# Applying the RMS factor behind the products at five layer boundaries of a three-model kernel

## The reference

```
def rms_norm_3(x, g):
    xf = x.astype(jnp.float32)
    y = xf * lax.rsqrt(jnp.mean(xf * xf, axis=-1, keepdims=True) + NORM_EPS)
    return (y * g.astype(jnp.float32)).astype(x.dtype)

def swiglu(h, w_gate, w_up, w_down):
    return (jax.nn.silu(h @ w_gate) * (h @ w_up)) @ w_down

    for layer in range(DEPTH):
        h = rms_norm_3(x, ffn1_norm[layer])
        x = x + FFN_RES * swiglu(h, ffn1_w_gate[layer], ffn1_w_up[layer], ffn1_w_down[layer])
        h = rms_norm_3(x, mix_norm[layer])
        ...
            proj = h @ ab_w_in[i]
        ...
        x = x + y
        h = rms_norm_3(x, ffn2_norm[layer])
        x = x + FFN_RES * swiglu(h, ffn2_w_gate[layer], ffn2_w_up[layer], ffn2_w_down[layer])
    return rms_norm_3(x, final_norm)
```

## Time and profile before

| | |
|---|---|
| time, median of 3 runs | 2904.82 us (2898.53 to 2907.13) |
| the profiled execution's own time | 2905.48 us |
| its span | 2902.9 us |
| PE busy | 2321.2 us, 80% |
| PE weight loads busy | 1765.4 us, 61% |
| DVE busy | 1185.5 us, 41% |
| ACT busy | 939.8 us, 32% |
| mean granted TensorE clock | 0.897 of full speed |
| HBM traffic | 687.09 MB read, 239 GB/s over the span |

### The profile page before, as it was taken

The page is one execution under the profiler, slowest core; times in us unless marked ns, Lnnn a source line. Parts: engine busy times, 40 slices in busy tenths (PEclk is TensorE's granted clock), DMA queues, the critical chain, the costliest instruction groups (busy, mean ns, idle before and its releaser), DMA issues. The chain is left out here.

```text
span 2902.9 us, 35108 instructions
## 1 busy us (share of the span) xinstructions
PE 2321.2 (80%) x14777; PEld 1765.4 (61%) x14777; DVE 1185.5 (41%) x1888; ACT 939.8 (32%) x1547; POOL 36.6 (1%) x50
## 2 busy tenths in 40 slices
PE   9875565557975566657988999999889999998998
PEld 7641111116741222117867877898779899887897
DVE  6620000026612000015665665555655455566554
ACT  5410000016510000003444444544544454434543
POOL 0010000000010000000000000000000000001000
PEclk9978778778988788877998999999999999989999
DMA  7199999993299999998222435555235555544452
GB/s 264 40 384 421 418 421 421 422 392 110 76 403 418 421 419 420 421 363 234 88 88 95 160 131 167 159 178 186 92 112 180 189 174 181 175 148 143 139 181 80
DMA packets 253356, 690.45 MB, mean 238 GB/s; under 512 B 38641, under 2 KB 137921, under 8 KB 203920
## 3 DMA queue, kind: packets, MB, share of 16 engines
q1 hardware_dynamic: 251920, 685.07, 63.7%
q0 software_dynamic: 1280, 3.15, 0.4%
HBM read 687.09 MB, written 5.28 MB: 239 GB/s over the span
## 5 line engine op out<-in xcount | busy, mean ns | idle before, releaser
L490 PE MATMUL accumulators<-xT_halves,weight_highs 128*128 128x256 f32 (+1 forms) x4400 | 810.6, 287 | 19.0 <-PEq L338 15.2
L249 DVE TENSOR_TENSOR weight_lows<-weight_ring,weight_highs 128x1024 fp32r<-128x1024 f32 (+1 forms) x504 | 603.4, 1214 | 462.8 <-ACT weight_highs L240 459.8
L490 PEld LDWEIGHTS accumulators<-xT_halves,weight_highs 128*128 128x128 f32 (+1 forms) x4400 | 692.1, 193 | 27.7 <-DVE weight_lows L249 14.4
L240 ACT CAST weight_highs<-weight_ring 128x1024 fp32r<-128x1024 f32 (+1 forms) x504 | 518.8, 1043 | 485.3 <-PE accumulators L490 470.8
L490 PE MATMUL accumulators<-xT_halves,weight_lows 128*128 128x256 f32 (+1 forms) x2200 | 627.3, 285 | 0.0
L1530 PE MATMUL accumulators<-weight_ring,arena 128*32 128x512 f32 x2048 | 318.6, 779 | 239.3 <-DMA weight_ring<-in_moe_w_up 127.8
L490 PEld LDWEIGHTS accumulators<-xT_halves,weight_lows 128*128 128x128 f32 (+1 forms) x2200 | 425.2, 193 | 0.5
L1530 PEld LDWEIGHTS accumulators<-weight_ring,arena 128*32 128x32 f32 x2048 | 86.1, 138 | 463.8 <-issue 463.8
L490 PE MATMUL accumulators<-weight_highs,arena_halves 128*128 128x512 f32 x1040 | 331.8, 396 | 12.4 <-PEq L338 5.4
L1530 PE MATMUL accumulators<-weight_ring,work 128*32 128x512 f32 x1024 | 161.2, 786 | 126.2 <-DMA weight_ring<-in_moe_w_down 123.6
L490 PEld LDWEIGHTS accumulators<-weight_highs,arena_halves 128*128 128x128 f32 x1040 | 198.6, 191 | 56.9 <-issue 11.9
(11 more groups left out here) (413 smaller groups left out, 1988.5 us busy)
## 6 DMA issues: line engine op xcount, KB each, us to landing
weight_ring<-in_moe_w_gate SPq DMA_DIRECT2D x128, 1024.0 KB, 19.8
weight_ring<-in_moe_w_up SPq DMA_DIRECT2D x128, 1024.0 KB, 20.5
weight_ring<-in_moe_w_down SPq DMA_DIRECT2D x128, 1024.0 KB, 20.6
weight_ring<-in_ffn_w_gate SPq DMA_DIRECT2D x44, 1024.0 KB, 5.3
weight_ring<-in_ffn_w_up SPq DMA_DIRECT2D x44, 1024.0 KB, 5.3
weight_ring<-in_ffn_w_down SPq DMA_DIRECT2D x44, 1024.0 KB, 4.9
weight_ring<-in_l_w_in SPq DMA_DIRECT2D x38, 1024.0 KB, 5.1
weight_ring<-in_l_w_out SPq DMA_DIRECT2D x14, 1024.0 KB, 4.9
```

Of the source, the lines that this page charges most:

```text
L240: act.copy(p.high(), p.raw()).then_inc(self.high_ready, 1)
L249: dve.tensor_tensor(p.low(), p.raw(), p.high().bitcast(F32), ALU.subtract).then_inc(self.low_ready, 1)
L490: last = pe.matmul(out, left[a], right[b], start=(start and i == 0), stop=(stop and i == 2), **kw)
```

## The change

A new tail, `LateTail`, takes the place of `RmsTail` at five of the seven turning tails: odd to ffn, ffn to pool_conv, pool_conv to ffn, ffn to ffn of the next layer, and selected attention to ffn. The tails into the odd layer, into selected attention and at the end stay.

- x is turned without its factor: PE transposes each chunk against the identity (16 transposes instead of 16 products with `diagonal`), in the order chunks 0 to 3 of t 0, of t 1, chunks 4 to 7 of t 0, of t 1. The high and low parts are made for both tiles at once, 8 times 256 columns instead of 16 times 128, and PE waits chunk by chunk.
- The factor is made behind that, for both tiles at once (`factor`), with a root, a reciprocal, two diagonals and half the factor (`halved`).
- `spread`: behind the next stage's first gate product (behind all of unit 0 in pool_conv) PE multiplies a matrix of ones by the two diagonals, which puts the 256 factors on every partition; DVE copies them to `rows_of` (`moved`).
- In the ffn a new DVE instruction per unit multiplies the gate bank by `rows_of` into `gate` (`scaled`), and ACT's Silu reads `gate` instead of PSUM. The up product keeps its factor out; the residual behind the down product multiplies by `halved` (a column of numbers) instead of 0.5.
- In pool_conv the three banks are left by DVE with a multiplication ("scaled") instead of by ACT's copy.
- `finish`, which every tail uses, makes tile 1 in another order: a and b of half 0, then a and b of half 1.

```diff
+class LateTail(RmsTail):
...
+    def pair(self, c):
+        bank = ((4, 5, 6, 7) if self.bank == 4 else (4, 5, 2, 3))[c // 2]
+        return self.m.ps[:, bank, c % 2 * T:c % 2 * T + T]
...
+    def tensor(self, pe, s):
+        rows_done = s["residual"] if self.final is None else s["normed"]
+        for g in range(2):
+            for t in range(TT):
+                if t == 0:
+                    pe.wait_ge(rows_done, 2)
+                else:
+                    pe.wait_ge(rows_done, 3 + g)
+                for c in range(DC // 2 * g, DC // 2 * (g + 1)):
+                    last = pe.transpose(self.pair(c)[:, t * P:(t + 1) * P], m.x[:, t, c * P:(c + 1) * P], m.const("ident"))
+                    if t == 1 and c % 2 == 1:
+                        last.then_inc(s["turned"], 1)
+
+    def spread(self, pe, spread):
+        pe.wait_ge(self.own["diagonal_ready"], TT)
+        for t in range(TT):
+            last = pe.matmul(m.ps[:, 6, t * P:(t + 1) * P], m.const("ones"), self.diagonal[t], start=True, stop=True)
+        last.then_inc(spread, 1)
...
+    def moved(self, dve, spread, spread_moved):
+        dve.wait_ge(spread, 1)
+        dve.tensor_copy(self.rows_of, self.m.ps[:, 6, 0:T]).then_inc(spread_moved, 1)
...
+        def high(c):
+            act.wait_ge(s["turned"], c // 2 + 1)
+            act.activation(self.m.xT_r[:, c, 0, :], self.pair(c), ACT.Copy, scale=gain[:, c:c + 1]).then_inc(s["scalar_moved"], 1)
...
+        def low(c):
+            dve.wait_ge(s["scalar_moved"], c // 2 * 2 + 2)
+            dve.scalar_tensor_tensor(self.m.xT_r[:, c, 1, :], self.pair(c), gain[:, c:c + 1],
...
@@ finish
-        for t in range(TT):
-            for h in range(2):
-                last = self.product(pe, a, t, h)
-            if t == 1:
+        for h in range(2):
+            self.product(pe, a, 0, h)
+        if ready:
+            ready()
+        for h in range(2):
+            self.product(pe, b, 0, h, True).then_inc(answered, 1)
+        for h in range(2):
+            last = self.product(pe, a, 1, h)
+            if h == 1:
                 last.then_inc(m.used, 1)
...
+            self.product(pe, b, 1, h, True).then_inc(m.used if h == 1 else answered, 1)
@@ ffn, PE
                         if part == 0:
-                            pe.wait_ge(s["silu_out"], u - 1)
+                            pe.wait_ge(s["scaled"], u - 1)
...
+                    if u == 0 and part == 0:
+                        late.spread(pe, s["spread"])
@@ ffn, ACT
-                gs.wait_used(act, 2 * u)
-                if u >= 2:
-                    act.wait_ge(s["hidden"], u - 1)
-                act.activation(gate[:, u % 2, :], m.ps[:, u % 2 * 2, :], ACT.Silu).then_inc(s["silu_out"], 1)
+                act.wait_ge(s["scaled"], u + 1)
+                act.activation(gate[:, u % 2, :], gate[:, u % 2, :], ACT.Silu).then_inc(s["silu_out"], 1)
@@ ffn, DVE
             for u in range(n):
+                m.lows(dve, gs.piece(4 * u + 2 + LEAD))
+                if u == 0:
+                    late.moved(dve, s["spread"], s["spread_moved"])
+                gs.wait_used(dve, 2 * u)
+                dve.tensor_tensor(gate[:, u % 2, :].rearrange("p (j t) -> p j t", j=2), m.ps[:, u % 2 * 2, :].rearrange("p (j t) -> p j t", j=2),
+                                  bview(late.rows_of, 1, 2), ALU.mult).then_inc(s["scaled"], 1)
                 m.lows(dve, gs.piece(4 * u + 4 + LEAD) - 1)
...
-            out.vector(dve, s, 0.5)
+            out.vector(dve, s, late.halved)
```

More of the change, by code:

```diff
@@ L560, in tensor, with residual @@
                         last.then_inc(s["turned"], 1)
+    def residual(self, dve, s, acc, add, last, t, h):
+        if t == 1 and h == 1:
+            last(dve)
+        else:
+            dve.wait_ge(s["answered"], 2 * t + h + 1)
+        by = add if isinstance(add, float) else add[:, t:t + 1]
+        dve.scalar_tensor_tensor(self.half(t, h), acc(t, h), by, self.half(t, h), ALU.mult, ALU.add).then_inc(s["residual"], 1)
     def warm_root(self, act, s):
@@ L3123, in ffn @@
     out = Out(m, ds, FFC, lambda c, t: [hT[:, k, c, t * P:(t + 1) * P] for k in range(2)], tail, 4)
+    late = m.late
     def half(k, u):
         return hT[:, k, 2 * u:2 * u + 2, :].rearrange("p c t -> p (c t)")
-    with m.stage("ffn", "silu_out", "hidden", "hidden_high", "hidden_low", *tail.names, joined=True) as (block, s):
+    with m.stage("ffn", "silu_out", "hidden", "hidden_high", "hidden_low", "scaled", "spread", "spread_moved", *tail.names, joined=True) as (block, s):
         @block.sync
@@ L3210, in pool_conv @@
     uT = ar[:, 3072:6144].rearrange("p (c t) -> p c t", c=12)
-    proj = Projection(m, in_stream, ("turned", "turned", "turned"), [uT[:, C * u:C * u + C, :] for u in range(3)])
-    with m.stage("pool_conv_in", *proj.names, joined=True) as (block, s):
+    late = m.late
+    proj = Projection(m, in_stream, ("scaled", "scaled", "scaled"), [uT[:, C * u:C * u + C, :] for u in range(3)], late.rows_of)
+    with m.stage("pool_conv_in", *proj.names, "spread", "spread_moved", joined=True) as (block, s):
         @block.sync
```

117 lines of the change are left out of this document (97 added, 20 removed).

## The result

The changed kernel takes 2883.91 us (median of 4 runs, 2882.2 to 2885.88) against 2904.80 us (4 runs, 2898.53 to 2907.13) for the kernel before: ratio 0.9937, 95% interval 0.9925 to 0.9948. That is 20.9 us less. The forecast was 2886, range 2879 to 2896.

What follows compares the result with a forecast made beforehand. PE was taken to bound the ffns, so only gaps between stages could be saved: 9.6 (three plain boundaries) + 3.8 + 5.8 = 19.2 us off 2905.5, less 0.7 for the median, gave 2886 us, range 2879 to 2896.

Steps and rivals of the forecast that it cites:

- 7.3 and 4.3 us behind the last product: Signs at odd to ffn and selected attention to ffn: when PE's first product on xT should come in the new trace.
- Start of the products at a plain boundary: At the three plain tails, PE starts the next stage's products 3.9 us sooner, 2.4 us after the first transpose.
- The spread: Behind each new tail, two float32 products added on PE's path cost 0.5 us, with 0.5 us of cover for the diagonals.
- Pacing of 0.2 us in an ffn: At an ffn's start, ACT's squares between high parts make chunk 4 0.1 to 0.2 us late; 0.2 us charged.
- ffn to pool_conv: Boundary gain of 3.2 us: 3.9 sooner, less 0.5 for the spread and 0.2 for DVE leaving pool_conv's third bank.
- The 0.2 us for leaving pool_conv by DVE: At pool_conv's third bank, DVE's multiplication takes 1.2 us against 1.01 for ACT's copy, costing 0.2 us.
- Odd to ffn: Boundary gain of 3.8 us: products 4.9 us sooner, less 0.6 for half clock and 0.5 for the spread.
- Selected attention to ffn: Boundary gain of 5.8 us: products 6.3 us sooner, less 0.5 for the spread, no fall of the clock assumed.
- The first: Rival: clock falls at every changed boundary because transposes don't hold it; costs 8.9 us, time 2894.5; chance 0.12.
- The second: Rival: ACT and DVE pace the first products, or diagonals delay the spread; 1 to 2 us per boundary, 2891 to 2895; chance 0.15.
- The third: Rival: in the ffn loop the gate's multiplication comes onto PE's path, 0.8 us per unit, 35 us, time 2921; chance 0.03.
- The fourth: Rival: less moves, as when PE passes slowly between stages' lists; 0.7 us each, 2889.5; chance 0.70 shared with the forecast.

Runs made afterwards that it cites:

- old_finish: The changed kernel with the old order of finish: 2887.26 us, ratio 0.9947 to the kernel before.
- four_plain: The changed kernel with the first four transposes at odd to ffn made as plain products with the identity: 2888.06 us, ratio 0.9947 to the kernel before.
- four_twice: The changed kernel with the first four transposes at odd to ffn each made twice: 2883.28 us, ratio 0.9936 to the kernel before.
- fewer_ahead: The changed kernel with two instead of four weight pieces made by DVE ahead of selected attention's last residual: 2882.33 us, ratio 0.9933 to the kernel before.
- three_plain: The changed kernel with the new tail only at the three plain boundaries, old tails at odd and selected attention to ffn: 2892.67 us, ratio 0.9959.
- spread_eight: The changed kernel with the spread's two products made eight times at each of the five boundaries: 2898.26 us, ratio 0.9975 to the kernel before.
- finish_alone: The kernel before with the new order of finish and nothing else: 2902.38 us, ratio 0.9995.
- gate_alone: The kernel before with one DVE multiplication of the gate bank by ones added per ffn unit: 2903.85 us, ratio 0.9997.
- after_again: The changed kernel run once more, no edit: 2886.36 us, ratio 0.9942 to the kernel before.
- plain_products: The changed kernel with the 16 transposes of each new tail replaced by plain products with the identity: 2890.20 us, ratio 0.9951 to the kernel before.

## Why the prediction was right, and where it wasn't

The direction, the mechanism and the size held: 19.2 us summed, 17.9 in the part that the change touches, 20.9 between the first medians and about 17 between the second. Over four traces with the old tails and five with the new ones (old_finish, four_plain and four_twice counted with after) that part gains 16.9 to 18.2 us, 1 to 2.3 less than summed; that the first medians lie beyond 19.2 is chance, from the stretch ahead of it. The prediction counts its 7.3 and 4.3 us behind the last product, and its 12.2 and 10.6 before, from about a quarter of a microsecond later than the rows do (the earlier trace rows give 12.45, 10.82); from start to start its forecasts are 7.55 and 4.55, and 7.39 and 4.58 were measured. By its own steps:

- **Start of the products at a plain boundary: right.** 3.9 us sooner forecast; 6.60 - 2.59 = 4.01. Behind the first transpose they come 2.35 us later (forecast 2.4).
- **The spread: right.** 0.5 forecast, 0.45 to 0.48 measured, on the path.
- **Pacing of 0.2 us in an ffn: wrong.** The only wait of PE for xT is the 0.45 us of the row above. 4.01 less 0.45 for the spread is 3.56, and that is what the two ffns gained, not 3.2.
- **ffn to pool_conv: 2.4 instead of 3.2.** PE kept 3.59 us of gain through the whole convolution: its output product started 98.26 us behind the ffn's last product before, 94.67 after. But then the clock came back later. The product's first instruction and the window in which the clock rose, before and then after:

```profile
2120.67 0.76 PE L490 MATMUL accumulators<-weight_highs,arena_halves 128*128 128x512 f32 x1 [5.39 <-PEq L338]
...
2123.00:2124.00 1.00, 1.00 (x5) 0.82 (x4) 0.00 (x0) 0.00 (x0) 0.00 (x0) 0.69 0.00 0
```

```profile
2108.15 0.77 PE L492 MATMUL accumulators<-weight_highs,arena_halves 128*128 128x512 f32 x1 [5.39 <-PEq L339]
...
2113.00:2114.00 1.00, 1.00 (x5) 0.82 (x4) 0.00 (x0) 0.29 (x1) 0.00 (x0) 0.68 0.00 0
```

  PE worked at half clock for 3.0 us before, for 5.5 after, behind the same wait of 5.39 us (a mean of 0.69 puts the rise 0.62 us into that microsecond). 2.5 us more at half cost 1.3 us, about the 3.59 - 2.40 = 1.2 that are missing. I had asked for the clock at the boundaries alone, not in the gaps inside the stages that the change shifts in time. The 0.2 us for leaving pool_conv by DVE can't be seen in the 3.59 (4.01 less 0.45 for the spread is 3.56). The missing 0.8 us belongs to the execution: fewer_ahead's edit lies behind this stretch, and yet the stretch is 1.2 us shorter there than in the changed kernel. It read 121.2 to 121.7 in four traces with the old tail and 117.7 to 118.9 in the seven with the new transposes and one spread, a gain of 2.3 to 4.0. In five of the seven the clock was back 5.5 to 5.9 us behind the product's start, in three_plain and fewer_ahead 4.3 and 3.4 us, and these two read 118.04 and 117.69.
- **Odd to ffn: 4.4 instead of 3.8.** The start was 5.06 us sooner (forecast 4.9); the clock cost less than the 0.6 charged (it was back at 1827, 0.6 us into the products, which costs 0.3). In fewer_ahead it was back 2 us later and this stretch read 195.38: the 0.6 lies within what this clock does from one execution to another. Over the traces an old tail read 198.9 to 199.6 here, a new one with transposes and one spread 194.5 to 195.4.
- **Selected attention to ffn: 5.7, forecast 5.8**, the clock staying at 1.00 as taken. But this gain depends on which trace of the old kernel is asked: the old tails' products started 10.82, 10.09, 9.08, 8.95 and 8.80 us behind the last one in five traces, and the stretch with an old tail read 203.5 to 205.5. Against the shortest the boundary is worth 3.6 us. So near a hit was luck: the trace that I predicted from is the one of the five in which the clock stayed at half longest behind this boundary (3.1 us lost, 1.4 to 1.7 in the others). Nor does this row stand by itself. I took DVE's residual to keep its place behind PE's last product. But DVE's queue sets it: the residual follows the low part of the last attention head's result and four weight pieces. DVE's timeline, before and then after:

```profile
2692.49 0.42 DVE L3419 TENSOR_TENSOR arena_halves<-accumulators,arena_halves 128x256 fp32r<-128x256 f32 x1 [1.44 <-ACT arena_halves L3412]
2693.43 4.63 DVE L249 TENSOR_TENSOR weight_lows<-weight_ring,weight_highs 128x1024 fp32r<-128x1024 f32 x4 [0.53 <-ACT weight_highs L240]
...
2675.71 0.42 DVE L3571 TENSOR_TENSOR arena_halves<-accumulators,arena_halves 128x256 fp32r<-128x256 f32 x1 [1.44 <-ACT arena_halves L3564]
```

  Counted from selected attention's start (the last product of the ffn ahead of it), these low parts stand at 162.7 and 164.4 us. The residual began at 168.1 to 168.3 us in the five traces with the old tail, whether PE's last product was at 167.6 or at 168.9; in the changed kernel it began at 169.9, later by the same 1.7 us as the low part. So the new transposes began 171.3 us behind that start, where the old turning products had (171.3 to 171.4). Selected attention's stage and this stretch have to be added up: 372.3 to 373.1 us with the old tail, 369.2 with the new one in the five traces named above, which is 3 to 4 us. Spread_eight, in whose trace the clock ran through that stage as in finish_alone, gate_alone and three_plain, gives the boundary alone: 370.7 less its 3.13 us of added spread is 367.6, against 372.3 to 372.4 in those three. That is 4.7 to 4.8 us, 1 less than forecast.
- **Not in the sum at all:** selected attention's stage, 1.7 us slower, and the odd layer's, 1.9 us faster. The change touches neither's products. In both the clock differs (the odd layer lost 9.3 and 6.6 us to it). Windows over one place of selected attention, before:

```profile
2552.00:2555.00 3.00, 3.00 (x22) 3.00 (x23) 1.23 (x1) 1.05 (x1) 0.00 (x0) 0.78 0.54 202
2555.00:2563.00 8.00, 8.00 (x40) 8.00 (x40) 1.31 (x2) 1.32 (x2) 0.00 (x0) 0.50 0.40 131
2563.00:2566.00 3.00, 3.00 (x23) 3.00 (x23) 1.20 (x1) 1.05 (x1) 0.00 (x0) 0.84 0.01 5
```

  The same place after:

```profile
2533.00:2536.00 3.00, 3.00 (x18) 3.00 (x18) 0.85 (x1) 1.04 (x1) 0.00 (x0) 0.58 0.77 275
2536.00:2546.00 10.00, 10.00 (x48) 10.00 (x49) 1.69 (x3) 1.31 (x2) 0.00 (x0) 0.50 0.34 109
2546.00:2549.00 3.00, 3.00 (x23) 3.00 (x23) 0.84 (x1) 1.05 (x1) 0.00 (x0) 0.81 0.02 7
```

  The clock is at half for 1.3 + 8 + 1.0 = 10.3 us before, and for 2.5 + 10 + 1.1 = 13.7 after: 3.4 us more at half, 1.7 us lost, which is the whole difference. The table's 9.2 and 10.0 differ by less, because some 80 us into the stage the clock was at half for 10.2 us before and 6.8 after; that doesn't show in the time, for after_again had 10.2 us there too and its stage read 169.33. Whether the new tails make the longer stretch likelier, by shifting the stage in time, is open: the kernels with the old tail behind selected attention read 167.6 to 168.9, those with the new one mostly 169.3, but 168.8 and 168.7 in spread_eight and fewer_ahead and 170.8 in plain_products. The odd layer read 248.4 to 249.6 in the three traces with the old `finish` and old tails, 247.6 to 249.1 in the eleven others, and the clock falls there at different places from one to the next.

**The rivals.** The first (the clock falls at every changed boundary) fell: 1.00 behind 16 transposes at all three plain boundaries and at selected attention, and equal with products in their place. The Trainium skill, TensorE: Matmul & The Clock Gate, Part 4: PE-mode transpose, says that the full clock doesn't engage for transposes, since they don't count as busy PE in the same way. These boundaries don't show it, but they hold only 1.9 us of transposes each; what stands against the page is the prediction's own row, the clock's rise at 1328 behind 3.65 us of transposes and nothing else. The second (pacing, 1 to 2 us per boundary) fell: one wait of 0.45 us, and no idle time at the spread, since the diagonals were ready 4.4 us behind the first product in an ffn and the spread came at 5.8 (a cover of 1.4 us, where 0.5 was forecast). The third (35 us slower) fell by gate_alone. The fourth wasn't needed.

**What no run separates.** The new tail is several edits in one. Of the 4.01 us at a plain boundary the wait for the second diagonal was 1.43, and transposes, which the late factor allows in place of products, bring 1.13 (plain_products). The other 1.45 us come with the rest: both tiles' parts made in one instruction per chunk, PE going on chunk by chunk, chunks 0 to 3 turned first. Whether the old tail would have gained that much by these alone, with its factor in place, was not run; so the 4 us are the whole tail's, not the late factor's alone.

## What to carry to other kernels

A per-row factor that commutes with a product can be moved behind it, and what it saves can be worked out beforehand: by how much the next stage's first product comes nearer to the last one, less every instruction that is added on the bound engine. Where another engine's queue sets the boundary, as at selected attention, add up the stage ahead of it as well. An added pass on an engine that is half idle costs nothing as long as its unit stays shorter than the bound engine's, which one experiment on the old kernel alone can show. Once such a boundary is short, look at what stands ahead of the residual on DVE's queue: two weight pieces less there gave up to 2 us more.

## What the runs showed of the hardware

- **The clock falls under work that the profile shows as 1.00 busy.** At one place of selected attention's stage PE was busy without a gap, and the clock still went to 0.50 for 10.3 us before and 13.7 us after (the windows above). The instructions there are products of 8 columns between those of 256. The trace after, just ahead of the fall and during it:

```profile
2533.10 0.25 PE L492 MATMUL accumulators<-weight_lows,xT_halves 128*128 128x8 f32 x1
2533.21 0.36 PE L492 MATMUL accumulators<-weight_highs,xT_halves 128*128 128x8 f32 x2
...
2535.76 0.77 PE L492 MATMUL accumulators<-xT_halves,weight_highs 128*128 128x256 f32 x2
```

  That the narrow products are the cause was only argued; no run took them away.
- **At the edge, the clock is a matter of the execution.** One kernel kept 1.00 across a wait of 2.29 us in one trace and fell to 0.50 in the next, worth 1.4 us. Differences of 1 to 2 us in a stretch with gaps of that length prove nothing by one trace; stretches without them (the two ffns behind plain boundaries) repeat to 0.02 us.
- **A transpose of 128 float32 columns leaves one record, a product two,** and costs half: 1.91 us for 16 against 3.73.
